# Second attention of a two-block transformer kernel: rounding and remainder of the joined output moved from POOL to ACT and DVE

## What is computed

```
logits = einsum("bnqhgd,bnkhd->bnhgqk", qb, kb) * (SW_HEAD_DIM ** -0.5)
logits = where(valid, logits, -inf)
m      = maximum(max(logits), sink)
pexp   = exp(logits - m)
probs  = pexp / (sum(pexp) + exp(sink - m))
out    = einsum("bnhgqk,bnkhd->bnqhgd", probs, vb)
...
merged = sigmoid(g_a) * (y_a @ w_branch_a) + sigmoid(g_b) * (y_b @ w_branch_b)
```

## Time and profile before

| | |
|---|---|
| median of 3 runs | 1884.35 us (1883.95 to 1885.29) |
| profiled execution, its time | 1884.16 us |
| its span (first to last instruction) | 1882.5 us |
| PE busy in the span | 1817.5 us, 97% |
| POOL busy | 886.1 us, 47% |
| DVE busy | 944.7 us, 50% |
| ACT busy | 774.0 us, 41% |
| the attention's loop | from 1263 to 1328 us of the span |

### The profile page before, as it was taken

The page is one execution under the profiler, slowest core; times in us unless marked ns, Lnnn a source line. Parts: engine busy times, 40 slices in busy tenths (PEclk is TensorE's granted clock), DMA queues, the critical chain, the costliest instruction groups (busy, mean ns, idle before and its releaser), DMA issues.

```text
span 1882.5 us, 24528 instructions
## 1 busy us (share of the span) xinstructions
PE 1817.5 (97%) x8928; PEld 1504.2 (80%) x8928; DVE 944.7 (50%) x1314; ACT 774.0 (41%) x1396; POOL 886.1 (47%) x667
## 2 busy tenths in 40 slices
PE   7889999999999999999999999999999999999997
PEld 5777878788888888888767888888788888888886
DVE  6255998644558841886662221238664321022436
ACT  5435888443542322224434332349324442133233
POOL 4134677475345444444532354448654444444442
PEclk9999999999999999999999999999999999999998
DMA  4321000243123233224222023220223222322321
GB/s 168 115 87 67 2 2 24 90 140 107 45 89 105 96 112 127 96 89 150 98 69 87 15 76 112 89 69 22 79 89 105 86 99 90 111 90 89 110 91 45
DMA packets 24269, 161.50 MB, mean 86 GB/s; under 512 B 2944, under 2 KB 3456, under 8 KB 5376
## 3 DMA queue, kind: packets, MB, share of 16 engines
q1 hardware_dynamic: 23184, 158.35, 24.6%
q10 hardware_dynamic: 1008, 2.12, 0.3%
HBM read 158.36 MB, written 2.10 MB: 85 GB/s over the span
## 4 chain that ended last, share of the span: by engine, by line
PE 88%; DVE 5%; ACT 3%; issue 2%; DMA 1%; POOL 0%; DVEq 0%; ACTq 0%; SPq 0%; POOLq 0%
PE psum L585 86%; PE psum L826 2%; DVE big_r L2032 1%; ACT w_hi_r L1220 1%; ACT big_r L1440 1%; PE psum L1134 1%; DVE acc L1953 0%; DVE h_lo L2057 0%; DMA xt<-in_x 0%; DVE tmp L1894 0%; DMA ring<-in_panels 0%; DVE big L2482 0%; ACT q_st L1694 0%; DVE negmax L2064 0%; ACT tmp L1694 0%
## 5 line engine op out<-in xcount | busy, mean ns | idle before, releaser
L2521 POOL TENSOR_TENSOR w_lo<-ring,w_hi_r 128x1024 fp32r<-128x1024 f32 (+2 forms) x268 | 639.9, 2409 | 772.1 <-ACT w_hi_r L1220 766.1
L585 PE MATMUL psum<-h_hi,w_hi_r 128*128 128x512 f32 x1200 | 472.5, 394 | 20.6 <-DVE h_lo L1947 10.1
L585 PE MATMUL psum<-big_r,w_hi_r 128*128 128x512 f32 (+1 forms) x1568 | 467.4, 381 | 5.1 <-DVE xt L1853 1.9
L585 PE MATMUL psum<-h_lo,w_hi_r 128*128 128x512 f32 x1200 | 469.7, 391 | 0.0
L585 PE MATMUL psum<-h_hi,w_lo 128*128 128x512 f32 x1200 | 469.4, 391 | 0.0
L1220 ACT CAST w_hi_r<-ring 128x1024 fp32r<-128x1024 f32 x286 | 283.9, 1042 | 379.8 <-PE psum L585 374.7
L585 PEld LDWEIGHTS psum<-big_r,w_hi_r 128*128 128x128 f32 x1568 | 289.7, 188 | 62.8 <-issue 4.4
L585 PE MATMUL psum<-big_r,w_lo 128*128 128x512 f32 (+1 forms) x784 | 298.3, 380 | 0.0
L585 PEld LDWEIGHTS psum<-h_hi,w_hi_r 128*128 128x128 f32 x1200 | 226.7, 189 | 71.7 <-issue 18.4
L585 PEld LDWEIGHTS psum<-h_hi,w_lo 128*128 128x128 f32 x1200 | 226.9, 189 | 47.9
L585 PEld LDWEIGHTS psum<-h_lo,w_hi_r 128*128 128x128 f32 x1200 | 227.0, 189 | 46.3
(11 more groups left out here) (347 smaller groups left out, 2524.7 us busy)
## 6 DMA issues: line engine op xcount, KB each, us to landing
ring<-in_panels SPq DMA_DIRECT2D x146, 1024.0 KB, 4.9
xt<-in_x SPq DMA_DIRECT2D x4, 512.0 KB, 8.8
out<-big SPq DMA_DIRECT2D x8, 256.0 KB, 2.2
ring<-in_panels SPq DMA_DIRECT2D x2, 512.0 KB, 7.1
big<-in_mem ACTq DMA_DIRECT2D x1, 1024.0 KB, 4.9
q_st<-in_ple ACTq DMA_DIRECT2D x1, 512.0 KB, 3.4
spare<-in_w_gate ACTq DMA_DIRECT2D x1, 192.0 KB, 7.0
spare<-in_w_k ACTq DMA_DIRECT2D x1, 128.0 KB, 9.2
```

The source lines that it names most:

```text
L585: return nc.tensor.matmul(o, l, r, start=start, stop=stop, **kw)
L2521: g.tensor_tensor(w_lo[:, p], ring[:, p], plain(w_hi[:, p]), ALU.subtract) \
```

## The change

`sw_store` is taken from POOL. Its rounding becomes `sw_store_hi` on ACT, its remainder `sw_store_low` on DVE. Both come one step later than before: at the second step after the odd unit of the pair is done, not the first. On ACT it stands at the end of the step, on DVE ahead of a join of the same step. The seventh of the eight falls into the last steps, the eighth behind the loop on both engines. Lines behind the new functions move: what was L1720 and L1724 on ACT is L1728 and L1732, what was L2356, L2361, L2366 and L2373 on DVE is L2364, L2369, L2374 and L2387, what was L2613 on POOL is L2630.

```
             for k in SW_STEPS:                              # ACT
                 if 0 <= k + LEAD - 1 < SW_NW:
                     sw_exp(sw_parts[k + LEAD - 1])
                 if k - 1 in sw_done:
                     sw_correction(sw_done[k - 1])
                 if 0 <= k < SW_NW:
                     sw_hi(sw_parts[k])
+                if k - 2 in sw_done and sw_done[k - 2] % 2:
+                    sw_store_hi(sw_done[k - 2] // 2)
+            sw_store_hi(len(sw_units) // 2 - 1)
...
+            def sw_store_hi(n):
+                act.wait_ge(sw["o"], 2 * n + 2)
+                nc.scalar.copy(sw_heads(sw_units[2 * n]["pair"], 0, sw_units[2 * n]["qt"]),
+                               nsa_o[n % 2].rearrange("p (h t) -> p h t", h=4)).then_inc(sw["o_hi"], 1)
...
+            def sw_store_low(n):
+                pair, qt = sw_units[2 * n]["pair"], sw_units[2 * n]["qt"]
+                dve.wait_ge(sw["o_hi"], n + 1)
+                V.tensor_tensor(sw_heads(pair, 1, qt), nsa_o[n % 2].rearrange("p (h t) -> p h t", h=4),
+                                sw_heads(pair, 0, qt, raw=True), ALU.subtract).then_inc(sw["o_lo"], 1)
...
                 if 0 <= k + LEAD - 1 < SW_NW:               # DVE
                     sw_coef(sw_parts[k + LEAD - 1])
+                if k - 2 in sw_done and sw_done[k - 2] % 2:
+                    sw_store_low(sw_done[k - 2] // 2)
                 if k - 1 in sw_done:
                     sw_join(sw_done[k - 1])
+            sw_store_low(len(sw_units) // 2 - 1)
...
-            def sw_store(n):                                # POOL
...
-                if k - 1 in sw_done and sw_done[k - 1] % 2:
-                    sw_store(sw_done[k - 1] // 2)
```

More of the change, by code:

```diff
@@ L2619, in sw_scale @@
                 last.then_inc(sw["scaled"], 1)
-            def sw_store(n):
[L2623 to L2629, removed]
             low(PAIR0["merge_b"], 1, (NARROW, PANEL))
```

## The result

| | before | changed |
|---|---|---|
| median | 1883.7 us (17 runs) | 1888.3 us (17 runs) |
| ratio | | 1.0025, 95% interval 1.0017 to 1.0034 |
| span of the profiled execution | 1882.5 us | 1886.6 us |
| the loop, from the first correction's start to the last one's | 45.00 us | 49.95 us |

One of the 17 executions before took 3676 us, about twice the others; the ratio is made from the fast ones alone, without it.

A forecast was written before the change was run, and what follows sets the result against it. PE, ACT and DVE run nearly abreast, ACT slightly ahead as the bound. Stores cost 1.2 + 1.84 + 4 x 1.2 = 7.84 us, less 0.53 for POOL: +7.3, giving 1891.7 us; range 1887.0 to 1894.5 us.

The forecast's parts named there:

- What bounds the kernel: Second attention's loop: PE, ACT and DVE nearly abreast, ACT slightly ahead with 0.10 us idle per pair, waiting in a ring.
- What ACT gets: Eight roundings of 128x512 within SBUF, each 0.63 us until done and 0.49 us until ACT goes on.
- What DVE gets: Subtractions of 128x512 from SBUF, each 0.69 to 1.23 us, because DVE waits out the POOL instruction under way.
- The walk at the first pair: First store in the loop: subtraction starts after POOL's second scaling, and ACT's exponential comes 1.2 us late.
- The walk at the third pair: Store where unit 6 comes due, POOL idle: join, remainder and maximum slip, and ACT's exponential starts 1.84 us late.
- The other four: Pairs 2, 4, 5 and 6: each between 0.84 and 1.5 us of delay, taken as 1.2 us.
- The 0.53 us less for POOL: Loop's end: PE's one wait for POOL, behind the seventh store, would vanish and save 0.53 us.
- What stands behind the loop: Exit: eighth subtraction ends some 4 us behind PE's last product, needed 11.5 us behind it, so it stays covered.
- Slack takes DVE's share: Rival, chance 0.12: DVE's wait and subtraction fall into idle time, only ACT's 0.49 us show; about +2.2 us, 1886.5 us.
- POOL held the loop: Rival, chance 0.05: POOL's freed time brings scalings early and pairs shrink to PE's 6.68 us; -2.0 us, 1882.3 us.
- The clock: Rival, chance 0.13: new gaps in PE lower its clock for four steps, 3.1 us more; +10.4 us, 1894.8 us.
- The marks listed: Signs expected in the changed profile, such as L1715 about 0.62 us and pairs of 7.5 to 8.2, plus signs of error.

The follow-up runs named there:

- the seventh experiment: The kernel before, all on POOL, with the sixth store moved behind the loop's last scaling: loop 44.95 us, median 1883.59 us, ratio 0.9997.
- the first experiment: The changed kernel with DVE's subtraction one step later still, same instructions on every engine: loop 46.50 us, median 1884.63 us, ratio 1.0008.
- the third experiment: The changed kernel with the rounding back on POOL one step ahead, only the remainder on DVE: loop 46.12 us, median 1884.73 us, ratio 1.0011.
- the second experiment: The changed kernel with the remainder back on POOL, only the rounding on ACT: loop 46.38 us, median 1884.41 us, ratio 1.0007.

## Why the forecast was right in sign and too large

**What bounds the kernel: right.** PE waits for DVE's remainder in the middle of the loop (4.4 us in five waits), ACT for DVE's maximum at the third pair, and both hang on DVE's wait for the rounding. The experiments show it by taking the wait away (4.95 to 1.50 us) and by putting one in (1.12 to 18.13, with the clock and the weight remainders in it). It is not the whole of it: at pairs 1 and 5 ACT's own instruction is the larger part, where the prediction's walk let it lie within DVE's delay.

**What ACT gets: right.** Eight L1715 of 0.634 us in the mean against 0.63; 0.52 us from start to start against 0.49. Alone it costs 1.38 us in the loop.

**What DVE gets: the price too high, because the order of starts was not asked for.** The prediction's sentence was that DVE waits until the POOL instruction under way is over, with a price between 0.69 and 1.23 us and, in the walk, a start only at the end of POOL's second scaling. In the loop the subtraction took 0.69 to 0.74 us, six times of six, and began when ACT was done; POOL's scaling is what gave way. The rule itself comes back where POOL's instruction had started well ahead. The timelines of POOL and of DVE at the seventh store, beside POOL's weight remainder:

```profile
1327.68 4.71 POOL L2555 TENSOR_TENSOR w_lo<-ring,w_hi_r 128x1024 fp32r<-128x1024 f32 x2
```

```profile
1331.55 1.39 DVE L2379 TENSOR_TENSOR big_r<-o_acc,big_r 128x512 fp32r<-128x512 f32 x1 [0.38 <-ACT big_r L1715]
...
1334.94 0.69 DVE L2379 TENSOR_TENSOR big_r<-o_acc,big_r 128x512 fp32r<-128x512 f32 x1 [0.69 <-ACT big_r L1715]
```

POOL's pair ends at 1332.39, the subtraction 0.55 us behind that. At the fourth store it is a scaling that had started first:

```profile
1309.92 1.52 POOL L2630 TENSOR_SCALAR q_st<-q_st,coef,ones 128x256 f32<-128x256 f32 x2 [1.19 <-DVE coef L2374]
```

```profile
1310.27 0.74 DVE L2379 TENSOR_TENSOR big_r<-o_acc,big_r 128x512 fp32r<-128x512 f32 x1 [0.45 <-ACT big_r L1715]
```

The first of the two scalings is over at 1310.47, the subtraction at 1311.01, 0.54 us behind: so little was left of the scaling that the wait cost 0.05 us. The second scaling is then the one that waits. Before shows both orders too, in the trace behind the earlier trace rows:

```profile
1344.97 0.69 DVE L2400 TENSOR_TENSOR tmp<-big,tmp 128x512 f32<-128x512 f32 x1
...
1348.23 2.77 DVE L1832 TENSOR_TENSOR big_r<-tmp,big_r 128x512 fp32r<-128x512 f32 x1
```

```profile
1345.37 5.09 POOL L2538 TENSOR_TENSOR w_lo<-ring,w_hi_r 128x1024 fp32r<-128x1024 f32 x2 [10.44 <-ACT w_hi_r L1220]
```

L2400 was beside L2538 as well, but it had started 0.40 us earlier, and it kept its 0.69 us; L1832 started 0.36 us behind the second L2538 and ended 0.55 us behind it. (The other L1832 of the earlier trace rows stood beside L2521, of the same form, and not L2538.) So the prices 0.69 and 2.77 differ by who started first, not by whether POOL was at work, and that is the step of the prediction that failed: it gave DVE the later place at every pair with POOL at work. The Trainium skill's rule, "GPSIMD Engine Reference", section 1 (Specifications), of a shared SBUF interface and contention with VectorE's two-input instructions, agrees with the stretched scalings (1.59 us for 1.08) as well as with the 1.39 us; what the prediction took from it, a price above 0.69 us for DVE wherever POOL is at work, does not hold for L2400.

**The walk at the first pair: mis-sized.** Predicted 1.2 us, measured 0.64. The walk had the subtraction start 1.04 us behind the start of ACT's L1715, 0.41 of that in waiting for POOL's second scaling; it started 0.68 us behind. That is 0.36 us of the difference. Another 0.13 is DVE's way from its remainder to the second maximum behind it, 2.19 us instead of 2.32.

**The walk at the third pair: right.** Predicted 1.84 us, measured 1.72; the walk had POOL idle there, which it was, so the failed step did not enter. Of the 0.12 us by which it was too large, 0.10 is the distance from subtraction to join, 0.61 us where the walk had 0.71.

**The other four: half right.** They were put at 1.2 us each, between 0.84 and 1.5, by carrying the first walk over. Measured: 0, 1.06, 0.80 and 0.78 us. That is 1.20, 0.14, 0.40 and 0.42 us less than booked, and the 1.20 of the second pair is the largest error of the sum. At the second pair ACT's rounding of the odd unit's last part (128x256) takes 0.37 us instead of 0.59 and DVE's maximum is over 512 columns instead of 260, so that L1715 is done at 1295.58 and DVE reaches its subtraction at 1295.62, with nothing to wait for. (At the sixth pair the part is as narrow, but DVE has no maximum left to make, reaches its subtraction earlier and waits 0.61 us.) And the time of the two new instructions falls into waits that before had there, of ACT for DVE's maximum and of DVE for a correction:

```profile
1295.79 0.47 ACT L1694 ACTIVATE tmp<-psum,negmax 128x256 f32<-128x256 f32 x1 [0.35 <-DVE negmax L2361]
```

```profile
1297.45 0.68 DVE L2373 TENSOR_TENSOR o_acc<-psum,acc 64x512 f32<-64x512 f32 x1 [0.44 <-ACT acc L1711]
```

Whoever carries a walk from one pair to another has to look at the widths of the parts and at the waits that are already there.

**The 0.53 us less for POOL: wrong.** They were called "the gain that rows vouch for". The seventh experiment frees PE of that wait and gains nothing. A row names the engine that came last; it does not say whether anything behind hangs on that wait. With the credit left out and the second store at nothing, the prediction's sum would be 7.84 - 1.2 = 6.64 us; with the measured 0.64 at the first pair, 1.72 at the third and 2.64 for the last three it is the 5.00 us found. The two errors have opposite signs: 2.84 us too much for the stores, 0.53 too much credit, so the sum missed by less than its parts.

**What stands behind the loop: right.** The last subtraction starts at 1334.94 and ends at 1335.63, 4.4 us behind PE's last product (1331.22), and PE first needs it 11.5 us behind that product. The exit cost nothing.

**The rivals.** Slack takes DVE's share (+2.2 us): not so for the whole, since five subtractions waited 3.7 us; but at pairs 1 and 5 (0.64 and 0.80 us) it is nearer than the forecast's 1.2, and it is what the first experiment turned the kernel into, at +1.50. POOL held the loop (-2.0): no; POOL's waits for DVE's coefficient grew from 5.0 to 16.8 us (1280 to 1328), and the loop gained nothing by the freed time. By the rule of "GPSIMD Engine Reference", section 4.1 (Engine selection), the Trainium skill puts such work on VectorE; the rows bear out its factor of two (1.29 and 0.69 us), and the kernel is still slower, as the third experiment is with DVE's part alone. The clock (+10.4): it does fall, and what that costs was overstated. It fell below 1.00 in one of three executions behind the gap of 1.86 us at unit 6 and cost nothing, because PE was not what was waited for; it fell in one of two executions of the kernel with the third store on POOL and cost 0.66 us, because there it was. The dip came in one execution of three; the price of 3.1 us did not come in any.

**The marks listed.** L1715 near 0.62: 0.62 to 0.65. Idle time of 0.5 to 1.3 us before L2379, put down to ACT, at each of the six in the loop: 0.45 to 1.24 at five, none at the second. L2379 between 0.69 and 1.23: seven of the eight. An exponential that waits for DVE's maximum: one, 1.15 us. A full pair of 7.5 to 8.2 us: 7.43, just under. The loop 7 to 8 us longer: 4.95. Two marks of being wrong came up. L2379 over 1.3 us did once, at 1.39, but it was for one POOL instruction and not for several: that one was 2.36 us long. The clock under 1.00 did in the first profile, and cost nothing.

**Still open.** In both kernels with ACT's rounding on time and DVE not waiting (the first and the second experiment) gap 13 is 1.50 us against 2.30 before, while gaps 7 and 8 are longer than before by 0.82 us in sum. Before, ACT waits 0.93 us for PE ahead of a rounding there; in those two it waits 0.17 or less. Of the 0.80 us, 0.51 is what gap 12 is longer by: the correction of unit 12 stands behind L1715 there, and PE's transposes do not, which come 0.51 us earlier when measured from that correction. What brings the other 0.3 about was not tried. No arrangement beat before; the seventh experiment equals it.

## What to carry to other kernels

In a loop where engines hand work round in a ring, what an added instruction costs is decided less by its length than by whether its input is ready when its engine gets to it: ask for the instruction ahead and the one behind, and leave a whole step between two moved instructions that feed each other. A wait in the profile names who came last, not what would be saved; before booking it as a gain, find what behind it would come earlier. And before using a contention price, look in its row at which of the two instructions had started first.

## What the runs showed of the hardware

- A subtraction of DVE with both inputs in SBUF (128x512) that starts ahead of an instruction of POOL keeps its 0.67 to 0.69 us, and POOL's instruction takes longer: a scaling (one tensor input) 0.91 instead of 0.55 us in the first experiment; a pair of weight remainders (two inputs) 5.09 us instead of 4.73 in before. Started 0.08 us behind a scaling it takes 0.72, and it is still the scaling that is stretched, to 1.06 us.
- If POOL's instruction has been under way for 0.35 us or more, the subtraction ends 0.54 to 0.56 us behind that instruction's end, whether it is a scaling (0.74 us, fourth store) or has two inputs: 1.39 us here, 2.77 in before, and 2.20 in the first experiment, where it started at 1327.77 and POOL's weight remainder ended at 1329.41. In the stores of these runs no start lies between 0.09 and 0.35 us behind POOL's, so where the one turns into the other is not shown.
- PE's granted clock fell to 0.50, behind a wait of 1.86 us, in one of three executions of one and the same kernel, and in one of two of the kernel with the third store on POOL. That such a gap brings it down is not certain from this, and a single profile can mislead either way.
